# Whole-block transposes, centred RWKV values, spare PSUM banks and a remade order in a one-core encoder layer

## What is computed

```python
h = rms_norm(x, norm_mix);  p_a, p_b, p_c, p_d = split(h @ w_in)
# A, RWKV-7, per token:  S = S * w_t + (S @ a_t) b_t^T + v_t k_t^T ;  y = S @ r_t
y = layer_norm_f32(y, ln_g, ln_b, RWKV_LN_EPS)      # over the 64 values of a head
out = (y + sum(r * k * r_k) * v) * silu(gate)
# B: causal depthwise conv of width 31;  C: HGRN2, chunks of 64 tokens;  D: stick-breaking attention
x = x + concatenate([y_a, y_b, y_c, y_d]) @ w_out
x = x + memory_cross_attention(rms_norm(x), rms_norm(mem), wq, wk, wv, wo)
return rms_norm(x, norm_final)
```

## Time and profile before

| | us |
|---|---|
| median of three runs | 1172.0 |
| the profiled execution | 1169.8 |
| its span, first to last instruction | 1168.0 |
| TensorE busy | 1082.0 (93%) |
| VectorE busy | 597.7 (51%) |
| ScalarE busy | 394.5 (34%) |
| GpSimd busy | 293.6 (25%) |
| mean granted clock of TensorE | 0.971 |

### The profile page before, as it was taken

The page is one execution under the profiler, slowest core; times in us unless marked ns, Lnnn a source line. Parts: engine busy times, 40 slices in busy tenths (PEclk is TensorE's granted clock), DMA queues, the critical chain, the costliest instruction groups (busy, mean ns, idle before and its releaser), DMA issues.

```text
span 1168.0 us, 26141 instructions
## 1 busy us (share of the span) xinstructions
PE 1082.0 (93%) x11316; PEld 929.1 (80%) x11316; DVE 597.7 (51%) x828; ACT 394.5 (34%) x673; POOL 293.6 (25%) x259
## 2 busy tenths in 40 slices
PE   6999979999989899999876999999979998999997
PEld 5787867976667797787764778788559988999997
DVE  5338998743648434424485764443351155446115
ACT  7304112133524211444544434354530053124023
POOL 3345543001125001224100200442053222342220
PEclk9899989999899999999988999999989999999999
DMA  6111211000101000011101005746641111121103
GB/s 228 37 31 42 55 36 38 4 3 11 28 19 45 12 5 20 19 36 46 46 2 37 20 19 175 235 146 200 202 137 62 37 38 37 38 64 46 36 19 145
DMA packets 84148, 71.76 MB, mean 61 GB/s; under 512 B 4097, under 2 KB 72897, under 8 KB 84034
## 3 DMA queue, kind: packets, MB, share of 16 engines
q1 hardware_dynamic: 84034, 70.09, 19.9%
HBM read 57.49 MB, written 12.58 MB: 60 GB/s over the span
## 4 chain that ended last, share of the span: by engine, by line
PE 69%; DVE 19%; ACT 8%; issue 2%; DMA 1%; POOL 1%; SPq 0%; DVEq 0%; ACTq 0%; POOLq 0%
PE units L1065 11%; PE bank L1330 8%; PE bank L1332 7%; PE bank L1331 7%; PE bank L1014 6%; DVE yT L1633 6%; PE bank L1015 5%; PE bank L1016 5%; PE bank L1054 3%; DVE A L1630 3%; PE bank L1049 2%; ACT B L1351 2%; ACT A L1351 2%; PE duo L1278 2%; DVE B L1939 1%
## 5 line engine op out<-in xcount | busy, mean ns | idle before, releaser
L1330 PE MATMUL bank<-vhi,act_hi 128*128 128x256 f32 x768 | 219.8, 286 | 14.3 <-DVE act_lo L1630 5.9
L1331 PE MATMUL bank<-vlo,act_hi 128*128 128x256 f32 x768 | 217.8, 284 | 0.0
L1332 PE MATMUL bank<-vhi,act_lo 128*128 128x256 f32 x768 | 217.6, 283 | 0.0
L1014 PE MATMUL bank<-act_hi,whi 128*128 128x512 f32 x464 | 196.0, 422 | 0.1
L1015 PE MATMUL bank<-act_lo,whi 128*128 128x512 f32 x464 | 185.7, 400 | 0.0
L1016 PE MATMUL bank<-act_hi,wlo 128*128 128x512 f32 x464 | 185.6, 400 | 0.0
L937 POOL TENSOR_SCALAR whi<-wraw 128x512 fp32r<-128x512 f32 x62 | 56.4, 910 | 492.8 <-PE bank L1016 384.5
L1065 PEld LDWEIGHTS units<-A 64*64 64x64 f32 x4608 | 146.0, 138 | 33.2 <-issue 13.7
L1065 PE MATMUL units<-A 64*64 64x64 f32 x4608 | 153.3, 223 | 20.5 <-DVE A L1788 8.4
L1330 PEld LDWEIGHTS bank<-vhi,act_hi 128*128 128x128 f32 x768 | 147.4, 192 | 16.5 <-DVE act_lo L1630 6.7
L1331 PEld LDWEIGHTS bank<-vlo,act_hi 128*128 128x128 f32 x768 | 147.6, 192 | 0.0
(11 more groups left out here) (171 smaller groups left out, 1543.6 us busy)
## 6 DMA issues: line engine op xcount, KB each, us to landing
wraw<-in_w_in SPq DMA_DIRECT2D x62, 256.0 KB, 2.9
A<-in_x SPq DMA_DIRECT2D x8, 512.0 KB, 8.1
x<-in_x SPq DMA_DIRECT2D x8, 512.0 KB, 7.8
moved<-in_wq SPq DMA_DIRECT2D x16, 256.0 KB, 5.1
keys_dram<-moved SPq DMA_DIRECT2D x16, 256.0 KB, 2.1
vals_dram<-moved SPq DMA_DIRECT2D x16, 256.0 KB, 2.2
vraw<-in_w_out SPq DMA_DIRECT2D x16, 256.0 KB, 2.7
vraw<-keys_dram SPq DMA_DIRECT2D x16, 256.0 KB, 2.7
```

The source lines that it names most:

```text
L1014: mm(bank, wh, act_hi[:, k, cols], start=k == 0, stop=False)
L1330: mm(bank, ah, vhi[:, (m + 1) % 2, k, :], start=k == 0, stop=False)
L1331: mm(bank, ah, wide_lo(m)[:, k, :], start=False, stop=False)
L1332: ins = mm(bank, al, vhi[:, (m + 1) % 2, k, :], start=False, stop=k == KT - 1)
```

## The change

1. Of the `tok` units, the 20 other than v become four transposes of 128x128 each. The bank then holds 128 tokens on the partitions, two chunks to a block, and has four readers of half the partitions: two copies on ScalarE and two on VectorE (for hv, four on ScalarE).
2. The v units stay pairs, but multiply by `centre` (identity less 1/64), so that the token-major values have no mean over the head. y is linear in them and comes out centred; `mu` is gone, and the square follows the copy in `yy`.
3. `hT` takes the ring `tn` in place of `pj`.
4. Token tiles 0 and 1 of the mixers' output are split into a buffer of their own, `ysp`, inside stage 2, after the three mixer ends; only ysplit 2 waits for the last weight tiles and the stores. The first four wide products take these two tiles for column blocks 0 and 1, with ysplit 2 to 7 between them. Six weight loads now go ahead of the last stores, two more among them.
5. The planner gets eight chains instead of four (cut, with the same dependencies), new weights, ranks, holds and `tok` costs; the order of stage 2 is another one.

```diff
@@ -58,21 +58,18 @@
...
-IDLE = 20.678
-URGENT = (22.606, 2883.263, 1.195, 2238509.171)
-AHEAD = 1.139
+IDLE = 60.0
+URGENT = (34.211, 64.887, 39.81, 53.8, 25.403, 0.241, 7.449, 7.673)
+AHEAD = 2.956
 PIECES_TOGETHER = 1
...
+HOLD = {('h', 1, 'f'): ('sbv', 0, 1, 5)}
...
         step(rec, ("bon", i), [("P", 1.1), ("D", 1.4)])
-        halves(rec, ("tok", "b", i), [("P", 1.1), ("A", 0.6)], lambda h: [("rwb", i)])
-        halves(rec, ("tok", "k", i), [("P", 1.1), ("A", 0.6)], lambda h: [("rwb", i)])
+        halves(rec, ("tok", "b", i), [("P", 0.55), ("A", 1.5)], lambda h: [("rwb", i)])
+        halves(rec, ("tok", "k", i), [("P", 0.55), ("A", 1.5)], lambda h: [("rwb", i)])
...
@@ -166,20 +163,19 @@
         for c in range(1, NC - 1):
             step(rec, ("cs", i, c), [("P", 0.12), ("D", 0.2)])
             if c in (NC // 2 - 2, NC - 2):
-                step(rec, ("yy", i, c // (NC // 2)), [("P", 2.8), ("A", 0.6)], ("cs", i, c))
-        step(rec, ("mu", i), [("P", 1.1), ("D", 1.4), ("A", 0.6)])
+                step(rec, ("yy", i, c // (NC // 2)), [("P", 2.8), ("A", 1.2)], ("cs", i, c))
...
+    for i in range(2):
+        step(stick, ("ysplit", i), [("A", 1.1), ("D", 1.4)], ("rfin", 1), ("hfin", 1), ("cfin",))
...
+    def cut(chain, *firsts):
+
+        at = [0] + [n for n, (stage, _, _) in enumerate(chain) if stage in firsts] + [len(chain)]
+        return [chain[a:b] for a, b in zip(at, at[1:])]
+
+    chains = cut(rec, ("lora", 1), ("hgate", 0), ("hgate", 1)) + [list(conv)] + cut(stick, ("sv", 1)) + [list(mem)]
...
@@ -392,8 +396,10 @@
     s.append(("derive",))
     s += mixer_order()
 
-    s += [("ysplit", i) for i in range(TT)]
-    s += [("wide", "o", n, i) for n in range(3) for i in range(TT)]
+    for i in range(4):
+        s += [("wide", "o", i // 2, i % 2), ("ysplit", i + 2)]
+    s += [("ysplit", 6), ("ysplit", 7)]
+    s += [("wide", "o", n, i) for n in range(3) for i in range(2 if n < 2 else 0, TT)]
...
@@ -619,9 +627,9 @@
             if name == "xT":
                 for q in range(2):
                     tn.plan((name,) + a + (q,), reads=2)
-            elif name in ("mT", "hT"):
+            elif name == "mT":
                 for q in range(2):
-                    pj.plan((name,) + a + (q,), reads=1 if name == "mT" else 2)
+                    pj.plan((name,) + a + (q,))
...
+            elif name == "tok":
+                rw.plan((name,) + a, reads=1 if a[0] == "v" else 4)
+            elif name in ("hdiag", "hlev", "hkv", "hout"):
                 rw.plan((name,) + a)
...
-            elif name == "pT":
+            elif name in ("hT", "pT"):
...
+
+        def turned(bank, dst, hd, odd):
+
+            to, of = slice(hd * HD, hd * HD + HD), slice(odd * CH, odd * CH + CH)
+            return (dst[to, :].rearrange("p (c o d) -> p c o d", o=2, d=HD)[:, :, odd, :],
+                    bank[of, :].rearrange("p (c e d) -> p c e d", e=2, d=HD)[:, :, hd, :])
...
+
+        def acts(name, i):
+
+            if name == "o" and i < 2:
+                return ysp[:, i, 0], ysp[:, i, 1]
+            return act_hi[:, :, i * P:(i + 1) * P], act_lo[:, :, i * P:(i + 1) * P]
...
@@ -876,14 +898,17 @@
             early = range(2 if x2_at < len(tiles) else 0)
             for u in early:
                 load_wide(u)
-            for n in range(len(tiles) - STORE_LAG, len(tiles)):
-                store(n)
             for i in range(max(0, len(tiles) - x2_at), TT):
                 load_x2(i)
-            for u in range(len(early), 2):
+            for u in range(len(early), 6):
                 load_wide(u)
-            load_wide(2)
-            load_wide(3)
+            last_unit = max(n for n, stage in enumerate(SCHED) if stage[0] in ("sbv", "hvar", "var", "cvar"))
+            freed = max(len(tiles) - 2, tiles_begun(SCHED[last_unit]) - 2)
+            for n in range(len(tiles) - STORE_LAG, len(tiles)):
+                if n == freed:
+                    for u in range(6, 8):
+                        load_wide(u)
+                store(n)
             for n, t in enumerate(tiles[-2:]):
...
-            load_wides(1, 12)
+            load_wides(2, 12)
...
-                pairs(bank, h, lambda r, col: src[r, col], lambda r, col: ident[r, r], post)
+                if kind == "v":
+                    pairs(bank, h, lambda r, col: src[r, col], lambda r, col: centre[r, :], post)
+                    return
+                for c in range(4 * h, 4 * h + 4):
+                    ins = tr(bank[:, (c - 4 * h) * P:(c - 4 * h + 1) * P], src[:, c * P:(c + 1) * P], ident)
+                post(ins)
...
-                tok_ = slice(i * P, (i + 1) * P)
+                hi, lo = acts(name, i)
...
+                bank = rw.rd_open(act, key)
+                for odd in range(2 if kind == "hv" else 1):
+                    for hd in range(2):
+                        nc.scalar.copy(*turned(bank, A[:, dst, hs(h)], hd, odd)).then_inc(rw.free(rw.units[key][0]), 1)
...
+                done(act, av(A[:, rP1, hs(h)], A[:, rkk, hs(h)], ACT.Square), "yc_sq")
...
                 if i == 0:
                     mixers_done(act)
+                elif i == 2:
                     for t in tiles[-2:]:
                         for h in range(2):
                             pj.rd_open(act, tuple(t) + (h,))
                     wait_stored(act, len(moves))
                 tok_ = slice(i * P, (i + 1) * P)
-                done(act, nc.scalar.copy(act_hi[:, :, tok_], yT[:, :, tok_]), "y_hi")
+                done(act, nc.scalar.copy(acts("o", i)[0], yT[:, :, tok_]), "y_hi")
...
+                ts(centre[:], eye[:], -1.0 / HD, None, ADD, name="centre_ready")
...
+            def tok(kind, p, h):
+                if kind in ("v", "hv"):
+                    return
+                key = ("tok", kind, p, h)
+                bank, dst = rw.rd_open(dve, key), {"b": rBt, "k": rKt, "hk": hKt, "a": rKKt}[kind]
+                for hd in range(2):
+                    V.tensor_copy(*turned(bank, A[:, dst, hs(h)], hd, 1)).then_inc(rw.free(rw.units[key][0]), 1)
...
-                tt(act_lo[:, :, tok_], yT[:, :, tok_], act_hi[:, :, tok_].bitcast(F32), SUB, "y_split")
+                hi, lo = acts("o", i)
+                tt(lo, yT[:, :, tok_], hi.bitcast(F32), SUB, "y_split")
```

More of the change, by code:

```diff
@@ L319, in read_out @@
         return [("A", 0.6)]
-    chains, pieces = [list(rec), list(conv), list(stick), list(mem)], [(t, 3, k) for t in (("xw",), FIRST_TILE) for k in range(KT)]
+    def cut(chain, *firsts):
+        at = [0] + [n for n, (stage, _, _) in enumerate(chain) if stage in firsts] + [len(chain)]
+        return [chain[a:b] for a, b in zip(at, at[1:])]
+    chains = cut(rec, ("lora", 1), ("hgate", 0), ("hgate", 1)) + [list(conv)] + cut(stick, ("sv", 1)) + [list(mem)]
+    pieces = [(t, 3, k) for t in (("xw",), FIRST_TILE) for k in range(KT)]
     supplied, tile_over = -SUPPLY, [-SUPPLY, 0.0]
@@ L473, in program @@
         eye = sb("eye", [P, CH])
+        centre = sb("centre", [P, CH])
         DC = sb("DC", [P, NC])
@@ L944, in _, with transposed @@
             heads = [slice(0, HD), slice(HD, P)]
-            def transposed(name, src, i, ring=pj):
+            def transposed(name, src, i, ring):
                 for q in range(2):
@@ L974, in mT @@
                 pe.wait_ge(sem("m_scaled"), i + 1)
-                transposed("mT", A[:, MEM_ROWS + i, :], i)
+                transposed("mT", A[:, MEM_ROWS + i, :], i, pj)
             def hT(i):
                 pe.wait_ge(sem("h_scaled"), i + 1)
-                transposed("hT", late[:, 2 + i % 2, :], i)
+                transposed("hT", late[:, 2 + i % 2, :], i, tn)
             def part(*a):
@@ L1320, in wide @@
                     elif name == "s":
[L1321 removed]
+                        tn.wait_read(pe, ("hT", i, 1))
                     else:
@@ L1496, in yy @@
                 copy_out(rw, ("yy", p, h), A[:, rkk, hs(h)])
-            def mu(p):
-                for h in range(2):
-                    rw.wait_read(act, ("mu", p, h))
-                    done(act, av(A[:, rP1, hs(h)], A[:, rkk, hs(h)], ACT.Square), "yc_sq")
+                done(act, av(A[:, rP1, hs(h)], A[:, rkk, hs(h)], ACT.Square), "yc_sq")
             def var(p):
@@ L1840, in cs @@
                                                        in1=A[:, rH, c * CH:(c + 1) * CH], op0=MUL, op1=ADD), ("cs", p, c))
-            def mu(p):
-                for h in range(2):
-                    bank = rw.rd_open(dve, ("mu", p, h))
-                    y = A[:, rkk, hs(h)]
-                    rw.rd_done(dve, V.scalar_tensor_tensor(out=y, in0=bank, scalar=-1.0 / HD, in1=y, op0=MUL,
-                                                           op1=ADD), ("mu", p, h))
             def rfin(p):
```

41 lines of the change are left out of this document (19 added, 22 removed), and 12 rows, old and new, of the table TILE_RANK.

## The result

| | before | after |
|---|---|---|
| median, us (runs) | 1172.85 (4) | 1140.8 (4) |
| lowest to highest | 1170.56 to 1174.24 | 1139.76 to 1144.73 |
| span of the profiled execution | 1168.0 | 1138.7 |
| mean granted clock | 0.971 | 0.973 |

The ratio is 0.9735, with a 95% interval of 0.9706 to 0.9763: 2.65% faster, 31 us of 1171. Where later runs are compared, their ratio to the kernel before is turned into us with 1171, the level of the kernel before in all of them.

A forecast was written before the change was run, and what follows sets the result against it. TensorE's instructions plus its gaps were taken as the bound. 10.1 + 3.8 + 8 + 6 + 8 - 3 = 32.9 us off 1169.8 gave 1136.9, plus 2.2 for the median: 1139 us, range 1113 to 1166.

The forecast's parts named there:

- Banks: Normalising stage, 938 to 980 us: with hT off `pj`, waits for its readers go; 6 us, bounds 2 and 7.6.
- Seam: Mixers to wide products, 855 to 880 us: early splits of two tiles bring 8 of 11.6 us, bounds 2 and 11.6.
- What was named as late next: At the seam: second column block's weights, 8.6 to 14 us on GpSimd against 5.6, and stores behind loads, 0 to 4.
- The page's rule on the port: At the seam, VectorE and GpSimd splits exclude each other; about 6 of the 8 us would be given back, sum 1145.
- Mean step: Eight `mu` products on TensorE go by centring the values: 3.8 us.
- Transposes, the work: Mixers' `tok` units: transposes for pairs save TensorE 0.63 us a unit, 16 units counted, 10.1 us.
- the rival of slow transposes: A unit costs as much as before, so the 10.1 us go: 1149 us, chance 0.04.
- Transposes, the readers: TensorE's waits in the two-bank ring for the turned blocks' copies cost 3 us; at best nothing, at worst 35.
- Order: Stage 2's new list, a held tile of 11.1 us filling the starved level phase: 8 us, bounds 25 gained and 10 lost.
- The slower rival: VectorE bounds the ring, every block copy behind a tap or scan: 35 us instead of 3, 1179 us, chance 0.07.

The follow-up runs named there:

- a3_tok: The kernel before with only the block transposes (20 units turned as whole blocks with four readers), old order: ratio 1.0047 to before, 5.5 us slower.
- c1: All edits with the old order, the two hk units of the first HGRN2 block moved ahead of the attention step before them: 1163.67 us, ratio 0.9937.

## Why the prediction was right, and where only the total was

The time, 1140.8 us, is 1.8 from the forecast of 1139, but that closeness is in part luck. Banks and seam did what the forecast said, for its reasons. The terms for the mean step, the readers and the order were each off, and came out near the forecast only together. By its terms:

- **Banks.** 6 forecast, 6.8 measured alone. The mechanism, the bounds and the size held.
- **Seam.** 8 forecast, 11.1 alone, inside the bounds of 2 and 11.6. What was named as late next is late, by 2.9 us in the changed kernel with the two together (1.8 and 1.1), where I had given back 3.6. By its rows the term is 9.1 (5.3 of the 11.6 lost lay behind the gap and went too), by the ratio 11.1. The page's rule on the port (the Trainium skill, SBUF — State Buffer, "Who interferes with whom") would have given the seam 2. As a statement on durations it was seen, 2.11 against 1.27 us; as a price it was not, since GpSimd's last units stood clear of VectorE's splits.
- **Mean step.** 3.8 forecast, 1.8 alone. The eight products went, and about half of their time came back as something else; where, no run shows. The step that failed is counting all 3.8 as if TensorE were the limit at every place of `mu`.
- **Transposes, the work.** 10.1 forecast, at 0.63 a unit for 16 units; 10.6 went for all 20, at 0.53 a unit. I had taken a unit as half of the row of eight in 1.03 us. Back to back that rate was seen again (594.94), but four by themselves took 0.60 to 0.65 us, and where the granted clock was 0.50, at 627, eight took 1.97. So the rival of slow transposes came true in small part and not as a whole, which needed all of the 10.1 to go. By the Trainium skill's figure of about 275 ns for a transpose in context (TensorE: Matmul & The Clock Gate, Part 4) it would have held. The trace has that figure as the duration of a single one, 273 ns in the median of the 80, but they overlap, and what counts in a sum is the distance from one to the next, 0.13 us in a row of eight. The recorded "the trace disagrees" compares these two different things.
- **Transposes, the readers.** 3 forecast, from the ring's waits for masked copies. This is the step that failed. In the old order the readers and the clock that fell with them cost about 16 us: 5.5 lost and some 10.5 not gained. In the new order 6.9 of the 10.6 arrive, so they cost 3.7, near the 3, but with intervals as wide as that figure. Whether it is the planner's new costs of 1.5 us that do this was not tried apart from its new weights.
- **Order.** 8 forecast for it, and it is 4.2 alone, 19.8 on top of the other four. This is one quantity with the term above: without the transposes the order is worth 4.6, so some 15 of its 19.8 are what it takes back from their readers. I had priced the two apart and the sum came out, since 7 + 8 is near -5.5 + 19.8. The hold that I took as the heart of the order is worth 12.9 us in the changed kernel and 6.0 in the old order, on both sides of the 8.
- **The slower rival** was the better guide for the old order: there the readers did cost more than the transposes brought. Its mechanism, each block copy behind a tap, was seen only in part. The old list has two taps of the convolution among the b and k units of block 0, the new one none, and in a3_tok TensorE waits there 1.7 us for copies that stand behind a tap of 1.40 us. The longest wait, 7.2 us, stood behind an attention step.

Left open: which of the new order's other moves make up the 14 us that the hold alone does not bring; how the readers' price splits into the bank's longer hold, the queues and the clock outside the places followed above; and where half of the mean step's time went.

## What to carry over

Price a new reader of a small bank ring in the order in which it will run: the same edit made the kernel 7 us faster or 5.5 slower by what stood around it. Where two serial chains run side by side and no filler work is left, the engine named by a wait is only the last of several: moving the named step ahead made the kernel slower in both orders, freeing the named engine gained 3 us there and lost more in other places, and work kept back for that stretch brought 6 and 13 us. An equal sum of waits under another name is no proof that nothing changed: compare them place by place. And separate an order from the edits it was made for before giving either a value, since alone it may show a fifth of its worth.

## What the runs showed of the hardware

A read out of PSUM over 64 partitions took as long as one over 128 with the same columns per partition: 0.367 against 0.377 us for copies on ScalarE, and 0.427 for a copy against 0.421 for an addition on VectorE. So cutting a block by partitions between two engines shortens neither engine's part. Each half of a turned block, as two instructions of 256 columns, cost 0.73 us on ScalarE or 0.85 on VectorE, where one copy of the whole bank had cost 0.586.

ScalarE and VectorE read the two halves of one bank at the same time (610.07 and 610.09 in c1) with no loss in either's duration: four copies in 1.55 and 1.80 us, against 1.54 and 1.80 in the changed kernel, where they did not meet.

A 128x128 transpose took 273 ns by itself, eight in a row 1.03 us at a granted clock of 1.00, the upper of TensorE's two levels, and 1.97 us at 0.50, the lower.
